# Prompt attention: values of two key heads in TensorE's column halves, sums of exponentials added on GpSimd, eight buffers of exponentials

## The reference

```python
def sparse_attend(q, k_sel, v_sel, valid):
    B, Q = q.shape[:2]
    qg = q.reshape(B, Q, N_KV_HEADS, Q_PER_KV, HEAD_DIM)
    s = jnp.einsum('bqngd,bqknd->bqngk', qg, k_sel).astype(jnp.float32) * (HEAD_DIM ** -0.5)
    s = jnp.where(valid[:, :, None, None, :], s, -jnp.inf)
    p = jax.nn.softmax(s, axis=-1).astype(v_sel.dtype)
    o = jnp.einsum('bqngk,bqknd->bqngd', p, v_sel)
    return o.reshape(B, Q, N_HEADS * HEAD_DIM)
```

## Time and profile before

| | |
|---|---|
| time, median of 3 runs | 6386.84 us |
| the profiled execution | 6381.06 us, span 6379.3 us |
| granted TensorE clock, mean | 0.854 |
| busy: TensorE, VectorE, ScalarE, GpSimd | 4882.5, 2275.0, 1870.2, 699.7 us |
| prompt attention | from about 722 to 2910 us |
| last casts of step 7 and of step 8 (L709) | 1939.7 and 2113.2 us |

### The profile page before, as it was taken

How to read it: one execution, slowest core, us unless ns; L and a number is a source line. 1 busy time by engine, 2 the same in 40 slices (tenths; PEclk the granted TensorE clock), 3 DMA queues, 4 the chain that set the end, 5 groups by cost and what they waited for, 6 DMA issues and landing times. The chain is left out here.

```text
span 6379.3 us, 58455 instructions
## 1 busy us (share of the span) xinstructions
PE 4882.5 (77%) x16452; PEld 2506.2 (39%) x16453; DVE 2275.0 (36%) x5015; ACT 1870.2 (29%) x3244; POOL 699.7 (11%) x900
## 2 busy tenths in 40 slices
PE   7999356777889998887675599936888886569980
PEld 2444122223333333333234444415565564534440
DVE  1111464445445546643122310134444442331105
ACT  0111134455666552221121122212222231212222
POOL 0111210000000000111221000120000000200013
PEclk9999577788999999998885699967898896579995
DMA  6111100000000000005342677771100100437865
GB/s 241 57 50 41 49 19 12 12 12 12 5 12 12 12 12 12 17 14 196 110 137 97 260 280 283 256 285 50 40 20 20 39 13 12 157 124 256 303 236 201
DMA packets 177186, 634.11 MB, mean 99 GB/s; under 512 B 28920, under 2 KB 47737, under 8 KB 157930
## 3 DMA queue, kind: packets, MB, share of 16 engines
q1 hardware_dynamic: 116764, 425.22, 19.0%
q0 software_dynamic: 39072, 131.90, 5.9%
q10 hardware_dynamic: 21184, 75.03, 2.9%
HBM read 497.41 MB, written 134.72 MB: 99 GB/s over the span
## 5 line engine op out<-in xcount | busy, mean ns | idle before, releaser
L2142 PE MATMUL experts_ps_gu<-w_sb,experts_xT 128*128 x1504 | 679.3, 606 | 43.9 <-DMA w_sb<-moe_w_in 39.4
L997 PE MATMUL attend_po<-attend_PT,V 128*128 128x512 f32 x1088 | 572.1, 652 | 8.9 <-ACT attend_total L742 8.9
L2659 PE MATMUL recurrent_psAB<-recurrent_hT,rec_w_in_sb 128*128 128x256 f32 (+1 forms) x2304 | 537.4, 393 | 10.6 <-ACT recurrent_hT L2454 10.6
L769 ACT ACTIVATE attend_passed<-attend_score,attend_cand 128x1024 bf16<-128x1024 f32 (+8 forms) x279 | 439.4, 1575 | 357.1 <-DVE attend_cand L869 333.3
L469 PE MATMUL project_pj<-project_w,project_hT 128*128 128x512 f32 (+2 forms) x1360 | 507.4, 531 | 6.6 <-ACT project_proj L385 5.5
L2659 PEld LDWEIGHTS recurrent_psAB<-recurrent_hT,rec_w_in_sb 128*128 128x128 f32 x2304 | 465.2, 216 | 76.7 <-issue 11.7
L1007 PE MATMUL attend_aux<-attend_hide,attend_identb 128*128 128x512 bf16 (+3 forms) x640 | 246.8, 389 | 291.0 <-DVE attend_mx L812 241.1
L812 DVE TENSOR_REDUCE attend_mx<-attend_aux 128x1 f32<-128x512 f32 (+3 forms) x640 | 365.2, 606 | 278.1 <-PE attend_aux L1008 270.7
L2142 PEld LDWEIGHTS experts_ps_gu<-w_sb,experts_xT 128*128 128x128 f32 x1504 | 285.4, 195 | 372.7 <-issue 372.7
L732 ACT ACTIVATE attend_PT<-attend_big 128x512 f32<-128x512 f32 x544 | 292.2, 588 | 366.0 <-PE attend_big L986 365.3
L2132 PE MATMUL experts_ps_y<-w_sb,experts_midT 128*128 x752 | 342.9, 599 | 11.4 <-issue 11.4
(11 more groups left out here) (425 smaller groups left out, 6132.3 us busy)
## 6 DMA issues: line engine op xcount, KB each, us to landing
w_sb<-moe_w_in SPq DMA_DIRECT2D x64, 2048.0 KB, 11.4
w_sb<-moe_w_in SPq DMA_DIRECT2D x64, 1024.0 KB, 8.8
yb_scratch<-experts_y ACTq DMA_DIRECT2D x94, 512.0 KB, 8.6
index_slab<-ada_w_in SPq DMA_DIRECT2D x12, 2048.0 KB, 12.1
sample_V<-cache_v_in POOLq DMA_DIRECT2D x128, 128.0 KB, 2.4
sample_K<-cache_k_in SPq DMA_DIRECT2D x128, 128.0 KB
route_x<-xa_scratch SPq DMA_DIRECT2D x32, 512.0 KB, 4.6
hs_scratch<-route_h ACTq DMA_DIRECT2D x32, 512.0 KB, 4.8
```

Source lines behind the costliest of these rows:

```text
L769: act.activation(passed[:, 0:L[m]], score[:, m % 2, 0:L[m]], ACT.Sign, bias=threshold, accum_out=balance[:, :]).then_inc(balanced, 1)
L997: pe.matmul(po[:, n % 2, :], V1[:, b, n, :], PT[:, g % 4, :], start=(b == 0), stop=(b == S[i] // NKV - 1)).then_inc(pv_done, 1)
L2142: last = pe.matmul(ps_gu[:, u, :], xT[:, u, k, :], w1[:, bass.ds(slot, 1), k, :].rearrange("p a n -> p (a n)"), start=(k == 0), stop=(k == ...
L2659: last = pe.matmul(psAB[:, c % 2, part, 0:W], w_in[:, k, part * D + c * P:part * D + (c + 1) * P], hT[:, k, 0:W], start=(k == 0), stop=(k ...
```

## The change

`V1` keeps 64 columns of values a head; the ones are gone (and their fill in the projection phase, and the place that the first phase borrowed in `V1` gets a buffer of its own). `with_values` now treats both heads of a slot: one head's matmul writes partitions 0 to 63 of bank j of `po`, the other's 64 to 127, each with 64 columns of weights at its own column position. Each half j of a step has its own bank.

The sums of the exponentials over the keys are made elsewhere: GpSimd adds every tile of exponentials to one of four accumulators `added_up` (the first of each head is copied), and at the end of each half `total_up` on TensorE multiplies the two accumulators by a matrix of ones, again in the column halves, into the same bank, after ScalarE has copied the values out of it. ScalarE then copies the sums (`copy_totals`). `PT` has eight buffers, and an exponential waits until GpSimd has added the tile that is eight back. GpSimd's other jobs of a step are set between the slots: `split_hide` ahead of slot 0, `spread_maxima` in the slot after the middle, `residual` one later, `narrow` at the end. `normalise` is spread from slot 2 on, not 1.

```diff
-        PT = sb("PT", [P, 4, 512])
+        PT = sb("PT", [P, DEEP, 512])
+        added_up = sb("added_up", [P, NKV, 512])
+        ones = sb("ones", [P, DH])
...
+        def totals_at(i, s):
+
+            second = [(i - 1, 1)] if there(i - 1) and s == min(1, middle(i)) else []
+            first = [(i, 0)] if there(i) and s == min(middle(i) + 1, slots(i) - 1) else []
+            return second + first
...
-            return share_of(5, s, 1, middle(i))
+            return share_of(5, s, 2, middle(i))
...
+                def add_exponentials(i, s):
+
+                    j, b = divmod(s, S[i] // NKV)
+                    for half in range(2):
+                        g = sum(S[:i]) + 2 * s + half
+                        acc = added_up[:, 2 * j + half, :]
+                        pool.wait_ge(exped, DEEP + g + 1)
+                        if b == 0:
+                            if i:
+                                pool.wait_ge(sums_done, 4 * i - 4 + 2 * j + half + 1)
+                            pool.tensor_copy(acc, PT[:, g % DEEP, :]).then_inc(added, 1)
+                        else:
+                            pool.wait_ge(added, sum(S[:i]) + 2 * s - 1 + half)
+                            pool.tensor_tensor(acc, acc, PT[:, g % DEEP, :], ALU.add).then_inc(added, 1)
+
                 for i in steps():
-                    if there(i + 1):
-                        split_hide(i + 1)
-                        spread_maxima(i + 1)
-                    if there(i - 1):
-                        residual(i - 1)
+                    n = slots(i)
+                    for s in range(n):
+                        if s == 0 and there(i + 1):
+                            split_hide(i + 1)
+                            pool.drain()
+                        if there(i):
+                            add_exponentials(i, s)
+                        if s == min(middle(i) + 1, n - 1) and there(i + 1):
+                            spread_maxima(i + 1)
+                            pool.drain()
+                        if s == min(middle(i) + 2, n - 1) and there(i - 1):
+                            residual(i - 1)
                     if there(i + 2):
                         narrow(i + 2)
+                        pool.drain()
...
-                        act.activation(PT[:, g % 4, :], big[:, g % 4, :], ACT.Exp).then_inc(exped, 1)
+                        if g >= DEEP:
+                            act.wait_ge(added, g + 1 - DEEP)
+                        act.activation(PT[:, g % DEEP, :], big[:, g % 4, :], ACT.Exp).then_inc(exped, 1)
...
+                def copy_totals(i, j):
+                    act.wait_ge(sums_done, 4 * i + 2 * j + 2)
+                    spread(total, j)
...
+                        if s == min(1, middle(i)) and there(i - 1):
+                            copy_totals(i - 1, 1)
...
-                    pe.wait_ge(exped, 4 + g + 1)
-                    if b == 0 and i + n // 2 > 0:
-
-                        pe.wait_ge(o_copied, 8 * (2 * i + n // 2))
-                    pe.matmul(po[:, n % 2, :], V1[:, b, n, :], PT[:, g % 4, :], start=(b == 0), stop=(b == S[i] // NKV - 1)).then_inc(pv_done, 1)
+                    pe.wait_ge(exped, DEEP + g + 2)
+                    if b == 0 and i:
+                        pe.wait_ge(o_copied, 16 * i - 8 + 8 * j)
+                    for half in range(2):
+                        pe.matmul(po[rows_of_half(half), j, :], V1[:, b, 2 * j + half, :], PT[:, (g + half) % DEEP, :],
+                                  start=(b == 0), stop=(b == S[i] // NKV - 1), tile_position=(0, half * DH)).then_inc(pv_done, 1)
+
+                def total_up(i, j):
+
+                    if i + j == 0:
+                        pe.wait_ge(ones_done, 1)
+                    pe.wait_ge(o_copied, 16 * i + 8 * j + 4)
+                    pe.wait_ge(added, sum(S[:i]) + (j + 1) * S[i] // 2)
+                    for half in range(2):
+                        pe.matmul(po[rows_of_half(half), j, :], ones[:, :], added_up[:, 2 * j + half, :],
+                                  start=True, stop=True, tile_position=(0, half * DH)).then_inc(sums_done, 1)
```

More of the change, by code:

```diff
@@ L543, in phase_attend @@
              "y_out", "consts", "spare"))
-        crossed, split_done, asked, balanced = (sem(n) for n in ("crossed", "split_done", "asked", "balanced"))
+        crossed, split_done, asked, balanced, added, sums_done, ones_done = (sem(n) for n in (
+            "crossed", "split_done", "asked", "balanced", "added", "sums_done", "ones_done"))
         TILE = [0] + list(range(1, NT, 2)) + list(range(NT - 2, 0, -2))
@@ L653, in _ @@
                 pool.memset(causal[:, :], 0.0).then_inc(consts, 1)
+                pool.memset(ones[:, :], 1.0).then_inc(ones_done, 1)
                 pool.wait_ge(consts, 1)
@@ L731, in exponentials, with spread, copy_out @@
                         act.wait_ge(pv_done, g + 1)
-                        act.activation(PT[:, g % 4, :], big[:, g % 4, :], ACT.Exp).then_inc(exped, 1)
-                def copy_out(i, j):
+                        if g >= DEEP:
+                            act.wait_ge(added, g + 1 - DEEP)
+                        act.activation(PT[:, g % DEEP, :], big[:, g % 4, :], ACT.Exp).then_inc(exped, 1)
+                def spread(dst, j):
                     for n in range(2):
-                        act.wait_ge(pv_done, 4 + sum(S[:i]) + (j + 1) * S[i] // 2 - (1 - n))
-                        heads = po[:, n, :].rearrange("p (h q) -> p h q", q=P)
+                        heads = po[rows_of_half(n), j, :].rearrange("p (h q) -> p h q", q=P)
                         at = (2 * j + n) * GQ // 2
                         for half in range(2):
-                            for dst, a in ((oT, 0), (total, DH)):
-                                act.activation(dst[half * DH:(half + 1) * DH, at:at + GQ // 2, :],
-                                               heads[a:a + DH, half:GQ:2, :], ACT.Copy).then_inc(o_copied, 1)
+                            act.activation(dst[rows_of_half(half), at:at + GQ // 2, :], heads[:, half:GQ:2, :], ACT.Copy).then_inc(o_copied, 1)
+                def copy_out(i, j):
+                    act.wait_ge(pv_done, DEEP + sum(S[:i]) + (j + 1) * S[i] // 2)
+                    spread(oT, j)
+                def copy_totals(i, j):
+                    act.wait_ge(sums_done, 4 * i + 2 * j + 2)
+                    spread(total, j)
                 def take_projection(i):
@@ L794, in _ @@
                             rectify(i + 3, pair)
+                        if s == min(middle(i) + 1, slots(i) - 1) and there(i):
+                            copy_totals(i, 0)
                         if there(i + 2) and by_act(i + 2):
@@ L1074, in _ @@
                             with_values(i, 2 * s - 2)
[L1075 removed]
                         elif there(i - 1):
                             with_values(i - 1, S[i - 1] - 2)
[L1078 removed]
                         for u in units[len(units) // 2:]:
                             fill(i + 1, u)
+                        for m, j in totals_at(i, s):
+                            total_up(m, j)
                         if s == middle(i):
@@ L2731, in build @@
             keep("kiT", [P, SEQ], until=attention)
-            keep("V1", [P, NT, NKV, P], until=attention)
+            keep("V1", [P, NT, NKV, DH], until=attention)
             with ExitStack() as projecting:
```

20 lines of the change are left out of this document (9 added, 11 removed).

## The result

The changed kernel takes 6543.31 us (median of four, 6539.44 to 6545.77) against 6385.18 (median of four): 158 us slower, ratio of the runs 1.0252, interval 1.0234 to 1.027. The forecast was 6342, its range ended at 6430.

A forecast was written before the change was run, and what follows sets the result against it. TensorE bounds the late second halves, the threshold search the early steps, VectorE step 11's first half. 98 - 26 - 8 + 5 - 6 - 20 = 43 us less than 6381.06: 6338, stated as 6342; range 6268 to 6430, the forecast's own 6310 to 6375.

The forecast's parts named there:

- The lock: Prompt attention: VectorE instructions with two SBUF inputs wait for GpSimd's two-input adds; 20 us on the path, bounds 0 and 127.
- the random-hit price of 127 us: Some 746 two-input VectorE instructions meeting GpSimd's adds at random, 0.17 us each: 127 us of VectorE's time.
- The second rival: VectorE's waits for GpSimd's adds decide, in search chain and second halves: 41 to 64 us slower, 6422; chance 0.21.
- The sign set for it: Threshold update L869's mean: 0.2 to 0.35 us forecast; above 0.5 with longer early steps would show the second rival.
- GpSimd's order and lag: GpSimd lags two to three slots behind bias and residual, delaying the cast of the queries: 6 us, bounds 0 and 40.
- Column halves: Value matmuls in pairs side by side: four take 1.16 us, saving 0.56 a slot; 98 us lands of 171.
- GpSimd's add: Each of 480 adds of exponentials takes about 1.2 us, bounds 1.17 and 2.34; with gaps about 700 us, which fits.
- the fourth rival: GpSimd becomes the bound, an add costing 2.34 us: 44 us slower, 6425; sign: exponentials' largest wait is for GpSimd; chance 0.08.
- The third rival: Column halves of the value matmuls run in turn, starting 0.43 us apart: 104 us slower, 6485; chance 0.07.
- Sums, copies and waits: Prompt attention: TensorE's sums cost 26 us, late copies on ScalarE 8, a removed wait of L997 gains 5.
- TensorE's busy time down by 110 to 150: Sign over the kernel: TensorE's busy time was to fall by 110 to 150 us.
- Outside the prompt attention: Sign for the rest of the kernel: nothing should move there.

The follow-up runs named there:

- 4: Changed kernel with its value matmuls at full width again, one head after the other, GpSimd still adding: 6565.03 us, ratio 1.0293.
- 8: Kernel of experiment 6, but with value matmuls at full width, one head after the other: 6473.79 us, ratio 1.0144.
- experiment 6: Changed kernel with GpSimd's program of before and the adds cut to one column on VectorE, sums left out: 6388.89 us, ratio 1.0013.
- experiment 1: Changed kernel with each of GpSimd's 480 adds made a single-input instruction on one column, sums left out: 6406.60 us, ratio 1.0044.
- experiment 3: Changed kernel with each of GpSimd's 480 adds made a single-input pass over the whole 128x512 tile, sums left out: 6472.66 us, ratio 1.0149.

## Why the prediction was wrong

Undone one after the other, the ends of the attention give a chain from before to after. Its terms depend on that order, as the 84 and 29 of experiments 4 and 8 show.

| step | us | the prediction's term |
|---|---|---|
| before to 8: sums by TensorE, later copies, eight buffers, VectorE's one-column work | +53.6 | +26 +8 -5 |
| 8 to 6: column halves | -84.2 | -98 |
| 6 to 1: GpSimd's new order, no adds; VectorE's one-column work goes (medians of the totals: +17.7) | +16.7 | part of +6 |
| 1 to 3: GpSimd busy with whole tiles | +71.3 | part of +6 |
| 3 to after: two inputs instead of one | +102.9 | +20 |

- **The lock, taken at 20 us: here it failed.** The mechanism was read rightly, in the main, out of the earlier trace rows, and the random-hit price of 127 us stood as the bound. The step from 127 to 20 was the mistake: "much stays hidden", since VectorE idles half of the stretch. It idles because it is a link in chains (search, indexer's scores, largest scores), and much of a wait in a link goes on to the next engine. Measured: 103 us at least on the path, and VectorE's time 228 us up. The random hit was too small too. Adds come in pairs behind each slot's exponentials and in runs behind a blocked GpSimd (eight in 9.81 us); and more than two-input instructions wait: L863 is a plain copy. The second rival had the cause, with 6422 for 6543. The sign set for it was on the wrong line: the updates' mean of 0.34 us lies in the forecast's 0.2 to 0.35, and the accumulation, for which no sign was set, lost the most (104 us).
- **GpSimd's order and lag, taken at 6: failed as well.** The prediction looked for the lag at the cast of the queries, where nothing came (60.3 before, 60.9 after). It didn't ask what VectorE does in the slots into which the bias and the residual were moved: it starts the indexer's scores, which then take 2.13 to 2.21 each in experiment 1. The 16.7 us of the table are a low figure, since the 69 us that VectorE worked for the sums in experiment 6 go in the same row, and setting both products sooner in the changed kernel gave 55 us back.
- **Column halves, 98: nearly right** where nobody adds (84), with four matmuls in 1.08 us, in the 1.0 to 1.15 forecast; 29 beside the adds. TensorE idles more, and its granted clock is lower where it does (1.00 to 0.92 in step 8's second half).
- **GpSimd's add, 1.2: right** (1.27), and GpSimd isn't the bound: the fourth rival's sign, the exponentials waiting for it, is 0.2 us. The third rival falls by the 1.08 us.
- **Sums, copies and waits, 29 us net: 54**, with VectorE's 240 one-column instructions and 32 whole first tiles in it (69 us of work), so not told apart.
- **TensorE's busy time down by 110 to 150:** 89 (4882.5 to 4793.9). L1029, unchanged, rose from 333.7 to 353.5 us at the lower granted clock.
- **Outside the prompt attention** nothing moved, as said: 3468 us from its end to the end of the span before, 3466 after.

The Trainium skill (TensorE: Matmul & The Clock Gate, Part 3, The mechanism) lets a weight load overlap matmuls in flight only if their row groups differ; here column halves share all rows, and four matmuls still took 1.08 us. The Trainium skill (GPSIMD Engine Reference, Key points) names the VectorE instructions that contend with GpSimd: those with two SBUF inputs, and those in a 2-port mode. For the first the trace agrees (the accumulation, 1043 ns for 670); whether the copy L863, with its 1.20 us, ran in such a mode no run here shows. On the inputs of GpSimd's own instruction that section says nothing, and experiment 3's 103 us hang on them.

## What to carry over

Before work goes to an idle GpSimd as two-input instructions in SBUF, list what VectorE runs at those moments and who waits for it, and charge each such instruction a good part of an add on the path: an engine that idles half its time inside a chain may hide little. A saving on one engine is worth its time only in the stretches which that engine bounds, so place the new work by stretch; here only the late second halves paid, and only with VectorE as the adder. GpSimd's jobs that are moved in the order need the same look as the new ones.

## What the runs showed of the hardware

- Two-input GpSimd adds run back to back shut a waiting VectorE instruction out until the queue has a gap: 8 adds and 11 adds (10.8 and 13.6 us). A gap of 0.16 us lets it in.
- What waited: two-input instructions on SBUF down to one element a partition, and one-input ones (L863, L976). What didn't: counting passes with an accumulated result (L897, 929 ns before and after) and reductions out of PSUM (L855, 614 ns in the prompt attention, before and after).
- GpSimd's one-input pass of 128x512 took 1.49 us, longer than its two-input add (1.27), and held VectorE off far less: updates that began beneath it had a median of 0.16 us (0.71 beneath an add), and the copy L863 took 0.61 at most (1.20).
- Float32 matmuls of 64 columns in the two column halves: four in 1.08 us, where four of 128 columns take 1.88.
